# Gate and pooled products in another order, and five embedding tiles per layer made at the norm and at the join

## The reference

```python
g_ssd, g_pool = jnp.split(jax.nn.sigmoid(gts), N_BRANCHES, axis=-1)     # gts = u @ w_in[:, 7200:9248]
mixed = (g_ssd * y_ssd + g_pool * y_pool) @ w_out[l]                    # y_pool = pooled mix @ w_br_pool
h = h + g1[:, None, :] * mixed
u2 = modulate(rmsnorm(h, norm_ffn_g[l]), sh2, sc2)
h = h + g2[:, None, :] * moe_ffn(u2, ...)
```

```python
h = h + rms_norm(y, norm_post[i])
e = p[i] @ ple_w[i]                     # (512 x 256) @ (256 x 1024): the embedding, known from the start
g = jax.nn.sigmoid(h @ ple_gate[i])
h = h + rms_norm(g * e, ple_norm[i])
```

## Time and profile before

| | us |
|---|---|
| median of 3 runs | 2762.91 (2761.85 to 2763.42) |
| profiled execution, its time | 2763.88 |
| profiled execution, its span | 2762.3 |
| TensorE busy | 2588.6 (94%) |
| VectorE busy | 1217.0 (44%) |
| ScalarE busy | 721.4 (26%) |
| mean granted clock of TensorE | 0.974 |

### The profile page before, as it was taken

How to read it: one execution, slowest core, us unless ns; L and a number is a source line. 1 busy time by engine, 2 the same in 40 slices (tenths; PEclk the granted TensorE clock), 3 DMA queues, 4 the chain that set the end, 5 groups by cost and what they waited for, 6 DMA issues and landing times. The chain is left out here.

```text
span 2762.3 us, 43676 instructions
## 1 busy us (share of the span) xinstructions
PE 2588.6 (94%) x17760; PEld 1690.1 (61%) x17760; DVE 1217.0 (44%) x2567; ACT 721.4 (26%) x1202; POOL 166.1 (6%) x128
## 2 busy tenths in 40 slices
PE   8999999999999899898999879999999998999997
PEld 3666666588765567566666538747877444555543
DVE  4666565757543222122222157416776224444422
ACT  2333332101113111111111111225554312444421
POOL 0000000000000022222222200000000000000000
PEclk9999999999999999999999989999999999999999
DMA  6222221243322789999998833431111311111110
GB/s 266 107 92 77 77 80 39 111 183 140 135 95 77 301 305 389 383 345 396 329 395 321 292 140 110 149 137 45 49 49 57 114 76 41 61 62 46 46 54 30
DMA packets 81430, 428.24 MB, mean 155 GB/s; under 512 B 16176, under 2 KB 16688, under 8 KB 38096
## 3 DMA queue, kind: packets, MB, share of 16 engines
q1 hardware_dynamic: 53296, 368.47, 34.0%
q0 software_dynamic: 18096, 37.80, 5.3%
q10 hardware_dynamic: 9840, 19.17, 1.9%
HBM read 394.88 MB, written 58.79 MB: 164 GB/s over the span
## 5 line engine op out<-in xcount | busy, mean ns | idle before, releaser
L284 PE MATMUL psum_all<-u,weights 128*128 128x512 f32 x720 | 314.6, 594 | 0.0
L284 PEld LDWEIGHTS psum_all<-u,weights 128*128 128x128 f32 x720 | 135.9, 191 | 162.0 <-issue 161.5
L1811 PE MATMUL psum_all<-weights,big 128*64 128x256 f32 (+2 forms) x1296 | 193.5, 402 | 12.0 <-DMA weights<-t_experts 12.0
L1811 PE MATMUL psum_all<-big 128*32 128x256 f32 (+2 forms) x1648 | 193.9, 382 | 9.5 <-DMA big<-t_experts 7.6
L954 PE MATMUL psum_all<-big,weights 128*128 128x256 f32 x768 | 176.3, 381 | 2.1 <-ACT sq L990 1.3
L1811 PEld LDWEIGHTS psum_all<-weights,big 128*64 128x64 f32 (+2 forms) x1296 | 135.5, 150 | 54.5 <-issue 20.6
L1811 PEld LDWEIGHTS psum_all<-big 128*32 128x32 f32 (+2 forms) x1648 | 136.4, 132 | 42.7 <-issue 11.6
L954 PEld LDWEIGHTS psum_all<-big,weights 128*128 128x128 f32 x768 | 144.7, 190 | 27.4 <-issue 5.1
L1846 DVE COPY big<-psum_all 128x256 f32<-128x256 f32 x46 | 19.5, 425 | 290.0 <-PE psum_all L294 290.0
L954 PE MATMUL psum_all<-big 128*128 128x256 f32 x624 | 141.8, 380 | 0.0
L284 PE MATMUL psum_all<-weights,u 128*128 128x256 f32 x640 | 139.6, 379 | 0.0
(11 more groups left out here) (443 smaller groups left out, 4015.1 us busy)
## 6 DMA issues: line engine op xcount, KB each, us to landing
big<-t_experts SPq DMA_DIRECT2D x96, 1024.0 KB, 28.2
weights<-t_experts SPq DMA_DIRECT2D x96, 1024.0 KB, 23.9
weights<-t_ada SPq DMA_DIRECT2D x24, 1024.0 KB, 7.1
weights<-t_rkvg SPq DMA_DIRECT2D x16, 1024.0 KB, 8.2
rwkv_inputs<-big ACTq DMA_DIRECT2D x48, 256.0 KB, 2.1
big<-rwkv_inputs SPq DMA_DIRECT2D x8, 1280.0 KB, 6.1
weights<-t_x SPq DMA_DIRECT2D x8, 1024.0 KB, 4.8
weights<-t_BC SPq DMA_DIRECT2D x8, 1024.0 KB, 5.1
```

Source lines behind the costliest of these rows:

```text
L284: last = pe.matmul(out, lhsT, rhs, start=n == 0, stop=n == len(terms) - 1)
L1811: ins = pe.matmul(K.psum[rows, bank, n * F_E:(n + 1) * F_E], xT[:, k, rows], X.part(r, n, KD, F_E)[:, k, :], start=k == 0, stop=k == KD - 1)
```

## The change

First, a function `seven_sum_late_pe` stands beside `seven_pe`. It has the same seven parts with the same operands and banks, in the order P1, P4, P7, P5, P6, P2, last product. The twelve units of the gate stage use it; the branch units and the recurrence's inputs keep `seven_pe`. ScalarE's order in the gate stage follows: the copy of P5 comes before the activation of the r1 quarter.

Second, embedding tiles 3 to 7 of each layer are made elsewhere, kept in DRAM and read back. Layer 0: two tiles behind the output products, one between the two sums of the norm, two behind the second sum; VectorE copies three before it waits for the root and two behind the scaling; SyncE stores them behind the row stores, and waits for the stores before the first expert load. Layer 1: weights and input are loaded behind the last expert weights into ring places 0 and 1; TensorE makes the five tiles ahead of the join's rows, ScalarE copies them, waits for both sets of rows and issues the stores; VectorE waits for the stores before its first scaled tile. At the end of a layer ScalarE's queue loads the five tiles back, and VectorE multiplies gate tiles 3 to 7 by them out of SBUF.

```diff
+def seven_sum_late_pe(K, q, n, R, key, B, Z, r1_read):
+    pe = K.nc.tensor
+    K.bank(Z.banks[0], *r1_read)
+    part(pe, Z.r1, B.b11, R.a11).then_inc(*q.pe.tick("P1", n))
+    pe.wait_ge(*q.dve.at("columns", n))
+    K.bank(Z.banks[1], q.dve, "c21", n)
+    part(pe, Z.r4, B.t4, R.a22).then_inc(*q.pe.tick("P4", n))
+    pe.wait_ge(*q.dve.at("s3", key))
+    K.bank(Z.banks[2], q.dve, "c12", n)
+    part(pe, Z.r7, B.t3, R.s3)
+    part(pe, Z.r5, B.t1, R.s1).then_inc(*q.pe.tick("P5", n))
+    pe.wait_ge(*q.dve.at("s2", key))
+    part(pe, Z.r6, B.t2, R.s2).then_inc(*q.pe.tick("P6", n))
+    pe.wait_ge(*q.act.at("p1", n))
+    part(pe, Z.r1, B.b21, R.a12, False).then_inc(*q.pe.tick("P2", n))
+    pe.wait_ge(*q.dve.at("s4", key))
+    pe.wait_ge(*q.act.at("p5", n))
+    return part(pe, Z.r5, B.b22, R.s4, False)
...
-    seven_pe(K, q, n, rows, key, C.unit(n), C.sets[n % 2], r1_read).then_inc(*K.W.left(i, q.pe))
+    seven_sum_late_pe(K, q, n, rows, key, C.unit(n), C.sets[n % 2], r1_read).then_inc(*K.W.left(i, q.pe))
...
-        if m < 2:
-            act.wait_ge(*q.pe.at("P2", n))
-            if j >= 2:
-                act.wait_ge(*q.dve.at("merged", j - 2))
-            act.activation(gate[0][:, 0:HALF], Z.r1, ACT.Sigmoid).then_inc(*q.act.tick("c11", n))
         p5_act(K, C, q, n, Z)
         if m == 2:
             continue
+        act.wait_ge(*q.pe.at("P2", n))
+        if j >= 2:
+            act.wait_ge(*q.dve.at("merged", j - 2))
+        act.activation(gate[0][:, 0:HALF], Z.r1, ACT.Sigmoid).then_inc(*q.act.tick("c11", n))
...
+def embed_sp(K, A, E, combined):
+    K.nc.sync.wait_ge(*combined.pe.all())
+    E.load_sp(K, A)
...
+def embed_store_sp(K, E, q):
+    for j in range(E.N):
+        sp.wait_ge(*q.dve.at("embed", j))
+        sp.dma_start(K.embedded[E.n, :, j, :], E.out[:, j, :]).then_inc(*E.stored.tick(j))
...
+    pe.wait_ge(*E.arrived.at("all_in"))
+    for j in range(2):
+        E.product_pe(K, q, j, EMBED_BANK[j], q.dve)
     pe_added_sum(K, q, "ffn", KD - 2)
+    E.product_pe(K, q, 2, EMBED_BANK[2], q.dve)
     pe_last_sum(K, q, "ffn", KD - 1)
+    for j in range(3, E.N):
+        E.product_pe(K, q, j, EMBED_BANK[j], q.dve)
...
+    for j in range(3):
+        E.copy_dve(K, q, j, EMBED_BANK[j])
+    dve.wait_ge(*q.act.at("ffn", "rstd"))
     modulated_dve(K, q, "norm_ffn_g", 32)
+    for j in range(3, E.N):
+        E.copy_dve(K, q, j, EMBED_BANK[j])
...
+    embed_store_sp(K, E, before)
     sp.wait_ge(*q.dve.at("order"))
+    sp.wait_ge(*E.stored.at(E.N - 1))
...
+def next_embed_sp(K, A, X, q, E):
+    for i in (len(ORDER) - X.RING, len(ORDER) - X.RING + 1):
+        sp.wait_ge(*part_left(q, i))
+    E.load_sp(K, A)
+def next_embed_pe(K, X, q, E):
+    K.nc.tensor.wait_ge(*E.arrived.at("all_in"))
+    for j in range(E.N):
+        E.product_pe(K, q, j, j, q.act)
+def next_embed_act(K, X, q, E, q_moe):
+    for i in range(len(ORDER) - X.RING + 2, len(ORDER) - X.RING + 4):
+        act.wait_ge(*part_left(q_moe, i))
+    for j in range(E.N):
+        E.copy_act(K, q, j, j)
+    for t in range(2 * NT):
+        act.wait_ge(*K.sums_in[t].at("in"))
+    for j in range(E.N):
+        act.wait_ge(*q.act.at("embed", j))
+        act.dma_start(K.embedded[E.n, :, j, :], E.out[:, j, :]).then_inc(*E.stored.tick(j))
...
+    dve.wait_ge(*K.embed_stored[1].all())
     dve.wait_ge(*before.act.at("next rstd"))
...
-        if j + 3 < KD:
-            embed(j + 3)
...
+    act.wait_ge(*K.embed_stored[n].all())
+    act.dma_start(X.embedded, K.embedded[n]).then_inc(*K.embed_back[n].tick())
...
-        dve.wait_ge(*(q.pe.at("embed", j) if j < KD - 1 else q.pe.at("w", w0 + 4)))
-        dve.tensor_tensor(X.out[:, j, :], X.sig[j % 2], K.psum[:, 2 + j % 5, :], ALU.mult).then_inc(*q.dve.tick("gated", j))
+        if j < Embedding.FIRST:
+            dve.wait_ge(*(q.pe.at("embed", j) if j < Embedding.FIRST - 1 else q.pe.at("w", w0 + 4)))
+            embedded = K.psum[:, 2 + j, :]
+        else:
+            dve.wait_ge(*K.embed_back[n].all())
+            embedded = X.embedded[:, j - Embedding.FIRST, :]
+        dve.tensor_tensor(X.out[:, j, :], X.sig[j % 2], embedded, ALU.mult).then_inc(*q.dve.tick("gated", j))
```

More of the change, by code:

```diff
@@ L1464, in part_left, with moe_sp @@
     return q.pe.at(("gate", "gate up", "down")[n], LAST_USE[r])
-def moe_sp(K, A, X, q, w0):
+def moe_sp(K, A, X, q, before, E, w0):
     sp = K.nc.sync
@@ L4263, in first_mixer, with experts @@
     w = K.W.take(4)
+    at = lambda a, n: K.big[:, a:a + n]
+    E = Embedding(K, 0, at(16 * T, 4 * T), at(20 * T, 2 * T), at(36 * T, 5 * T).rearrange("p (k t) -> p k t", t=T))
     residual_sp(K, A, w)
-    residual_pe(K, C, q4, q3, w)
-    residual_dve(K, q4, q3, w)
+    embed_sp(K, A, E, q3)
+    residual_pe(K, C, q4, q3, w, E)
+    residual_dve(K, q4, q3, w, E)
     residual_act(K, q4)
-    return q4
-def experts(K, A, before):
+    return q4, E
+def experts(K, A, before, E):
     q, qx = Steps(K, "moe"), TurnSteps(K)
@@ L4274, in experts @@
     X, w = Moe(K), K.W.take(4)
-    moe_sp(K, A, X, q, w)
+    assert 36 * T >= X.ring_at and X.ring_at + 12288 >= 41 * T
+    moe_sp(K, A, X, q, before, E, w)
     moe_pe(K, X, q, before, w)
```

48 lines of the change are left out of this document (42 added, 6 removed).

## The result

| | before | after |
|---|---|---|
| median of the first comparison, us | 2762.91 (2761.85 to 2763.42) | 2738.95 (2729.10, 2738.95, 2739.92) |
| ratio, 95% interval | | 0.9895 (0.9859 to 0.9932) |
| median of the second comparison, us | 2764.36 (13 runs, 2757.12 to 2774.05) | 2728.40 (5 runs, 2724.22 to 2730.45) |
| ratio, 95% interval | | 0.9872 (0.9849 to 0.9895) |
| span of the profiled execution, us | 2762.3 | 2727.8 |

The change makes the kernel faster, by 24 us in the first comparison and by 36 in the second. The profiled execution of after is the one of 2729.10 us. Two of its first three runs took 10 us more; in the profiled one the sum came out to 0.1 us (2762.3 - 2727.8 = 34.5, forecast 34.4).

The account below looks back on a forecast made before the run. TensorE, busy 94% of the span, was taken to bound the kernel. Terms -22.0 - 17.2 + 3.8 + 1.0 = -34.4 us took 2762.9 to 2728.5 us; own range 2723 to 2734, with rivals 1 to 3 2720 to 2741.

Parts of the forecast that it names:

- Part A: Gate stage: P2 moved behind P6 removes four TensorE waits for the first product's copy and the slow clock behind them, -22.0 us.
- the clock's part: Gate stage: 7.69 us of slow clock behind the four waits, claimed to go once the waits go.
- Rival 1: Gate stage: copy still late, or a short wait still lowers the clock; 7.3 us back, 2736 us; chance 0.11.
- Part B in the gate loops: Gate loops of both layers: removing five embedding tiles of 1.72 us saves 8.6 us a layer, 17.2 in two.
- Rival 5: Gate loops bound by something other than TensorE, so 17.2 us isn't given back; 2746 us; chance 0.03.
- Norm: Layer 0's norm: tiles ahead of the second sum lengthen the path; +3.8 us, bounds 3.5 and 5.5.
- Rival 4: Wait for the five stores holds up the first expert load; slower than before, 2765 us or more; chance 0.02.
- Join: Layer 1's join: the new load may delay GpSimd's adds and the second set of rows; +1.0 us.
- the bound of 4: Join: upper bound of its cost, if the first of the last three adds takes the longest landing time.
- rival 2: Join and stores collide: adds land later, 1.0 becomes 4 to 8 us, time about 2734; chance 0.11.
- The 3 us more: Join: by the skill's rule the embedding load takes from GpSimd's adds; the sum would lie 3 us higher.
- Rival 3: Join gains: TensorE's clock could still be full at 1604, work there shorter; 2725 us; chance 0.09.

Follow-up runs that it names:

- experiment 5: Changed kernel with P2 one place earlier, between P5 and P6, in each gate and pooled unit; 2727.98 us, one execution.
- experiment 6: Changed kernel with P2 two places earlier, between P7 and P5, in each gate and pooled unit; 2737.81 us, one execution.
- experiment 9: Changed kernel with the sigmoid of a gate unit's first half back in its old place on ScalarE, ahead of the copy of P5; 2735.41 us, one execution.
- experiment 2: Kernel before with only the gate stage's new order, all embedding tiles left in the gate loops; 2744.36 us, ratio 0.9922.
- experiment 4: Changed kernel with one embedding tile between the two sums of layer 0's norm, none ahead and four behind; 2725.56 us.
- experiment 8: Kernel of experiment 4 with VectorE's copies of tiles 1 to 4 moved behind its modulated inputs; 2728.06 us.
- experiment 7: Changed kernel with the join's 1 MB of embedding weights loaded three times, one after the other; 2738.09 us, one execution.
- experiment 3: Kernel before with only the five embedding tiles of each layer moved, gate stage in its old order; 2749.86 us, ratio 0.9945.

## Why the prediction was right, and where it wasn't

**Part A: -22.0 forecast, -22.00 measured.** The margins of the working (0.8 us in the first group, 1.9 in the others) are those of the trace, 0.82 and 1.93 in the first two groups. That the clock's part goes with the waits holds too. Rival 1 (a short wait still takes the clock down) had the wrong mechanism: waits of 0.77 to 2.41 us did not, in experiments 5, 6 and 9. Its price of 7.3 us for one late group was too high by that: a wait of 0.8 would have cost 1.0.

**Part B in the gate loops: -8.6 per layer forecast, -8.56 and -8.58 measured.** The stage of layer 1 moves by 0.5 with the attention in it; from the norm ahead of its gate loop to the end of the kernel it is 94.65 or 94.67 us with all tiles in the loop and 86.07 to 86.09 with five moved, 8.6 less in every profile. Rival 5 is out; steps without a tile take 6.9 us.

**Norm: +3.8 forecast, +3.74 measured.** The 72.38 behind it repeats in eight profiles, but the 68.64 that it is taken from is one profile. Against experiment 2, which has no tiles at the norm either and whose clock fell at another point, the cost is 72.38 - 69.39 = +2.99. So the mechanism is right, and agreement to 0.1 is luck. L325 stands 2.6 us behind L318, as in the working. What the working passed over is VectorE: the copies of tiles 0 to 2 stand ahead of its wait for the root. In this order they are over before the root comes (841.2 against 844.0), but they are the next thing late as soon as the tiles are put better, and hold the path by 1.5 us in experiment 4, of which experiment 8 got 0.6 back, because there they stand ahead of the router's eviction instead. The order that I costed is not the best one: only 1.67 us are idle between the two sums, so one tile belongs there and none ahead. Rival 4 is out: the stores land by 872 at the latest, 24 us ahead of the first expert load, which doesn't move.

**Join: +1.0 forecast.** The profiled execution has +0.44; in the twelve profiles with the tiles at the join its stage is 55.70 in the mean (54.75 to 56.94), in the two without 55.85 and 55.04. A cost that can't be told from nothing; neither the bound of 4 nor rival 2 was reached. The new 1.5 MB landed 3.8 us behind the last expert weights (1555.5 and 1551.7), as the working has it (4 us). The second set is loaded 0.16 us later against the last down product (16.78 and 16.62). The Trainium skill, "DMA: Bandwidth & Descriptors", section "Issuing engines are not separate DMA queues", has it that transfers started by different engines run on the same 16 DMA engines and interleave. The 3 us more that the working made of that rule did not come: the stage is no longer, and the last three adds of experiment 7 are no slower with 2 MB beside them. Whether the transfers interleave, no run here tells. TensorE's part was a little off: the tiles begin 1.5 us behind the load of the first set, not with it, and the rows are turned 1.9 us late, not 1. It has no effect, as the working says, and they are turned at full clock (4.07 us for 6.30). Rival 3 didn't come: the clock is at 0.50 again in 1585 to 1590, behind the wait of 4.03 for the second set.

**The sum** is right for a single execution, but the first median, 2738.95, lay 10.4 us above it: outside the forecast's own range of 2723 to 2734, inside that of the rivals (2720 to 2741), and near the 2736 of rival 1, whose late copy no profile shows. The second comparison gave 2728.40 and a difference of -36.0. The working took the spread of three runs of the kernel before (1.6 us) for its noise; thirteen runs spread over 17. Two sources of scatter of that size are seen: the experts' stage (8 us) and the clock at the end of the recurrence (10 us). Whether the second is what sets the kernel before's long runs apart is not known; they have no profile. Neither is a term of the change.

**Left open.** Whether the two runs of 2739 had the fall of experiment 7: their mean clock, 0.975 and 0.976 against 0.981, is lower by 0.005, which is what 27.3 us at half speed make of 2728 (27.3 x 0.5 / 2728 = 0.005), but they have no profile. Also why the experts' stage moves by 8 us, and whether filling the waits keeps the clock up.

## What to carry to other kernels

When an accumulating product waits for a copy of its own bank's first half, put the other products of the unit between the two, and move the reader of that bank on the copying engine along with it: here the product's move alone would have left 8.6 us. Work for an engine's idle time is free only if it stands behind the instruction that the path waits for, and if its own evictions don't stand ahead of the path's on another engine. Compare stage lengths, not only total times: here three changed stages repeated to 0.02 us while totals scattered by 17. But compare with more than one profile of the old kernel, too: its norm alone differed by 0.75 between two.

## What the chip showed that I had not expected

- The same program takes its clock down in a place of short waits in some executions only. At the end of the recurrence, with TensorE busy about 20 of 25 us and no wait over 1.03 us, 12 of the 13 profiles with the woven products (two of them filled) show 1.00 and one shows 0.50 for 27 us (+10 us). In another place of the recurrence (1937) one of 14 has it at 0.50 for 3.4 us. The Trainium skill, "TensorE: Matmul & The Clock Gate", section "What's actually happening", has it that the gate's sampling runs freely and is not tied to the kernel's start. That fits; no run here shows the mechanism itself.
- Single waits of up to 2.41 us between dense products left the clock at 1.00 (13 of them in experiments 5, 6 and 9); of eight waits of 3.1 to 4.3 us (before and experiment 3) six lowered it, for up to 3 us of extra time each.
- A 1 MB load beside GpSimd's last three adds took 5.6 to 6.2 us, and these adds were no slower than without it. Queued behind expert weights, the same load took 25 to 27 us to land.
